# The second piece of a long score row takes the first piece's minimum as its start, and each exponential waits for the reads of its own map

## The reference

```python
def block(args):
    qi, st = args
    sc = jnp.einsum('bhmqd,bhmkd->bhmqk', qi, k).astype(jnp.float32) * scale
    mask = kpos[None, :] <= (st + jnp.arange(Q_BLOCK))[:, None]
    p = jax.nn.softmax(jnp.where(mask, sc, -jnp.inf), axis=-1)
    a = p[:, :, 0] - lam * p[:, :, 1]
    return jnp.einsum('bhqk,bhkd->bhqd', a.astype(v.dtype), v)
```

## Time and profile before

| | us |
|---|---|
| median of the runs | 2307.16 |
| lowest and highest of the 3 | 2304.96, 2308.73 |
| the profiled execution | 2303.62 |
| its span | 2301.7 |
| PE busy in the span | 2207.7 |
| DVE busy | 1846.1 |
| ACT busy | 1121.8 |
| attention, 499 to 845 us of the span | 346.0 |
| PE busy in it | 310.7 |

### The profile page before, as it was taken

How to read it: one execution, slowest core, us unless ns; L and a number is a source line. 1 busy time by engine, 2 the same in 40 slices (tenths; PEclk the granted TensorE clock), 3 DMA queues, 4 the chain that set the end, 5 groups by cost and what they waited for, 6 DMA issues and landing times. The chain is left out here.

```text
span 2301.7 us, 29815 instructions
## 1 busy us (share of the span) xinstructions
PE 2207.7 (96%) x11258; PEld 1853.9 (81%) x11258; DVE 1846.1 (80%) x2593; ACT 1121.8 (49%) x1787; POOL 358.6 (16%) x285
## 2 busy tenths in 40 slices
PE   7999999987999999999999999998999999999998
PEld 4988897866889888878888788887887888878887
DVE  6548796989989886788888998877687777898887
ACT  4532554448888864433334545443343333545452
POOL 0343043833455640000000000000000000000000
PEclk9999999989999999999999999999999999999999
DMA  7441435130000035268888543447234444743434
GB/s 270 160 160 47 147 119 165 37 106 28 15 15 24 10 125 178 88 224 290 280 282 305 184 169 133 173 152 250 101 119 143 154 154 155 255 161 137 169 137 174
DMA packets 185738, 345.10 MB, mean 150 GB/s; under 512 B 11496, under 2 KB 83452, under 8 KB 184572
## 3 DMA queue, kind: packets, MB, share of 16 engines
q1 hardware_dynamic: 185508, 343.16, 43.9%
q10 hardware_dynamic: 88, 0.04, 0.0%
HBM read 236.20 MB, written 106.95 MB: 149 GB/s over the span
## 5 line engine op out<-in xcount | busy, mean ns | idle before, releaser
L2952 PE MATMUL ps<-sb_h_hi 128*128 128x512 f32 x512 | 200.1, 391 | 7.9 <-ACT ps L1710 2.6
L2954 PE MATMUL ps<-sb_h_hi,sb_h_lo 128*128 128x512 f32 x512 | 199.3, 389 | 0.0
L2953 PE MATMUL ps<-sb_h_lo,sb_h_hi 128*128 128x512 f32 x512 | 199.2, 389 | 0.0
L2918 PE MATMUL ps<-sb_h_hi,sb_w_hi 128*128 128x512 f32 x448 | 176.8, 395 | 9.1 <-DVE sb_u_full L2425 9.0
L2601 PE MATMUL ps<-sb_h_hi,sb_w_hi 128*128 128x512 f32 x448 | 177.4, 396 | 0.7 <-DVE sb_w_lo L2235 0.7
L2919 PE MATMUL ps<-sb_h_lo,sb_w_hi 128*128 128x512 f32 x448 | 175.4, 392 | 0.0
L2603 PE MATMUL ps<-sb_h_hi,sb_w_lo 128*128 128x512 f32 x448 | 174.5, 389 | 0.0
L2602 PE MATMUL ps<-sb_h_lo,sb_w_hi 128*128 128x512 f32 x448 | 174.4, 389 | 0.0
L2116 DVE TENSOR_SCALAR_CACHE_REDUCE sb_scores<-ps 128x1024 f32<-128x1024 f32 (+7 forms) x160 | 139.6, 891 | 12.4 <-PE ps L2815 6.9
L2952 PE MATMUL ps<-sb_w_hi 128*128 128x512 f32 x384 | 149.4, 389 | 0.0
L2953 PE MATMUL ps<-sb_w_lo,sb_w_hi 128*128 128x512 f32 x384 | 149.4, 389 | 0.0
(11 more groups left out here) (342 smaller groups left out, 5924.3 us busy)
## 6 DMA issues: line engine op xcount, KB each, us to landing
left_scratch<-sb_u_sum SPq DMA_DIRECT2D x128, 256.0 KB, 5.9
sb_right<-w_gated_scratch SPq DMA_DIRECT2D x16, 2048.0 KB, 8.7
sb_h_lo_full<-left_scratch SPq DMA_DIRECT2D x64, 512.0 KB, 3.8
sb_w_full<-in_w_ff SPq DMA_DIRECT2D x28, 1024.0 KB, 6.3
left_scratch<-sb_u_full SPq DMA_DIRECT2D x96, 256.0 KB, 2.3
sb_w_full<-left_scratch SPq DMA_DIRECT2D x48, 512.0 KB, 3.3
sb_w_raw<-in_w_in SPq DMA_DIRECT2D x16, 1024.0 KB, 6.0
sb_ada<-in_w_ada SPq DMA_DIRECT2D x32, 512.0 KB, 5.3
```

What stands on the lines that cost most here:

```text
L2918: M(psum[:, bank, :], wh[:, k, :], rh[:, k, :], start=fresh and k == 0, stop=False, skip_group_check=True)
L2952: M(dst, hi[:, k, tok], hi[:, 2 + k, :], start=fresh and k == 0, stop=False, skip_group_check=True)
L2953: M(dst, hi[:, k, tok], low[:, 2 + k, :], start=False, stop=False, skip_group_check=True)
L2954: ins = M(dst, low[:, k, tok], hi[:, 2 + k, :], start=False, stop=k == 1, skip_group_check=True)
```

## The change

Three things change.

- In a long unit the read of the second piece passes the first piece's minimum (`part_min[:, s, m, 0:1]`) as the initial value of its own minimum, so that `part_min[:, s, m, 1:2]` is the minimum of the whole row. Since that value is written by an earlier DVE instruction, the read now waits for `sc_read` to have counted it.
- The `TENSOR_REDUCE` into `row_min`, its wait, the tile and the semaphore `max_ready` are gone. `row_shift` takes piece 1 of a long row and piece 0 of a short one.
- Both exponentials of every unit wait for `sc_read`, each for the items of its own map: map 0 for all but the second half of the unit's items, map 1 for all of them.

```diff
         def row_shift(u, m):
 
-            return row_min[:, u % 8, m:m + 1] if u >= FULL else part_min[:, u % 8, m, 0:1]
+            last = int((u // HEADS + 1) * P > WIDE)
+            return part_min[:, u % 8, m, last:last + 1]
+
+        def scores_read(u, m):
+
+            return SC_NO[u + 1] - (0 if m else len(sc_items(u)) // 2)
...
             def exp_of(u, m):
                 n = (u // HEADS + 1) * P
-                if m == 0:
-                    if u < FULL:
-                        act.wait_ge(sc_read, SC_NO[u + 1])
-                    else:
-                        act.wait_ge(max_ready, u - FULL + 1)
+                act.wait_ge(sc_read, scores_read(u, m))
                 A(prob(u, m, 0, n), prob(u, m, 0, n), ACT.Exp, scale=-1.0, bias=row_shift(u, m),
                   accum_out=row_sum(u, m)).then_inc(exp_done, 1)
...
                     else:
+                        begin = None
+                        if c0:
+                            dve.wait_ge(sc_read, r)
+                            begin = part_min[:, s, m, 0:1]
                         dve.wait_ge(sc_mm, r + 1)
-                        V.tensor_scalar(prob(u, m, c0, n), sc_pair(r)[:, 0:n], -SCALE, None, ALU.mult, ALU.min,
+                        V.tensor_scalar(prob(u, m, c0, n), sc_pair(r)[:, 0:n], -SCALE, begin, ALU.mult, ALU.min,
                                         accum_out=part_min[:, s, m, c0 // WIDE:c0 // WIDE + 1]).then_inc(sc_read, 1)
                     r += 1
-                if u >= FULL:
-                    dve.wait_ge(sc_read, SC_NO[u + 1])
-                    V.tensor_reduce(out=row_min[:, s, :], axis=AX.X, op=ALU.min,
-                                    in_=part_min[:, s, :, :]).then_inc(max_ready, 1)
```

More of the change, by code:

```diff
@@ L302, in trunk @@
         part_min = sb("part_min", 207, [P, 8, 2, 2])
-        row_min = sb("row_min", 207.125, [P, 8, 2])
         exp_sum = sb("exp_sum", 207.25, [P, 4, 2, HEADS])
@@ L375, in trunk @@
         split_hi, split_lo = sem("split_hi"), sem("split_lo")
-        sc_mm, sc_read, max_ready, exp_done, a_ready = [sem(n) for n in (
-            "sc_mm", "sc_read", "max_ready", "exp_done", "a_ready")]
+        sc_mm, sc_read, exp_done, a_ready = [sem(n) for n in (
+            "sc_mm", "sc_read", "exp_done", "a_ready")]
         at_mm, at_read, pv_mm, o_read = [sem(n) for n in ("at_mm", "at_read", "pv_mm", "o_read")]
```

## The result

The changed kernel takes 2312.48 us (median of 20 runs, 2306.58 to 2318.28) against 2307.75 us (20 runs, 2300.78 to 2311.39) for the kernel before, run beside it: 4.7 us more. The kernel is slower by more than the 0.2% that can be told. The forecast was 2308.0 us, and its range ended at 2312.

The account below looks back on a forecast made before the run. It took PE or DVE, by stretch, as the limit, with 12.7 us of PE idle in the long units. Terms -1.0 + 0.8 + 0.5 + 1.1 - 0.5 = +0.9 us on 2307.2 gave about 2308.0 us, range 2299 to 2312.

Parts of the forecast that it names:

- the stretches with PE full: Attention at 690 to 737 us and 780 to 822 us: added or saved DVE time meets PE's queue, not its idle time.
- The reduce that goes: End of long units on DVE: 3 reduces at 737 to 780 us on the path, 0.33 us each, 1.0 us gained.
- the bound of 10 us: Upper bound on the removed reduces' gain: 0.33 us of DVE time in each of 32 long units.
- The operand and the wait: Map 0's second piece, 616 to 690 us: operand +0.8, wait +0.5; three units on DVE's path at 737 to 780: +1.1 us.
- The exponentials: Map 0's exponential on ACT starts earlier, may save part of a stall at crowded steps: -0.5 us, bounds 0 and 7.5.
- Rival 1: ACT's lead reaches PE: its turn-read waits except one of 2.0 us go, with one POOL collision; about 2300 us; chance 0.15.
- what can't be summed: `combine`'s small operation takes 1.48 us beside POOL, 0.22 alone; two such shifts allowed, 2.5 us on either side.
- Rival 3: Map 0's second piece, every long unit: start value 0.21 us plus wait 0.12 in the loop; +7, 2314 us; chance 0.13.
- Rival 2: DVE's time is the path and waits are free, outside the stretches with PE full: -3.6, 2303.5 us; chance 0.08.
- The rule against the row: Added waits on DVE: free by the skill's rule, sum 1.2 us lower; 0.12 us each by the trace row, which was used.
- What was to show it: Profile after: no L2121, second pieces 0.06 to 0.07 us longer, ACT's waits under 3 us, long units within 2 us of 206.
- The two signs named as proof of being wrong: 616 to 690 us shrinking by more than 2 us, or second pieces longer by 0.15 us or more.

## Why the prediction was wrong

Two steps failed. The sum charged the start values' operand and wait in too few units, because it took the stretches with PE full as a cover; that is 1.4 us. And it had no term for the granted clock behind PE's waits; that is the larger part of what is left. Of the mechanism, the reduce, the prices and the place in the loop were right. As a difference the forecast was +0.9 us and its range ended at +4.8 over the 2307.16 us of then; the median moved by 4.7 us. So as a difference it is at the range's very end and as a time, 2312.48 us, just above it, where no term of the sum had put it.

**The reduce that goes, -1.0 us.** Right in kind: the loop of the earlier trace rows passes beside it, and the bound of 10 us was far off. Measured -0.5 us in 24 units, and -0.8 us with units 56 and 60 to 62, close to the 1.0 us.

**The operand and the wait, +0.8, +0.5 and +1.1 us.** The prices were right, 0.065 and 0.11 to 0.12 us. So was the place: map 0's second piece is in the loop, map 1's is beside it. The number of units was wrong, and this is the first step that failed. I charged 13 units of 616 to 690 us (they reach n = 1536, not 1408) and 3 later ones, and took the stretches with PE full as a cover. The runs showed 3.0 us in 24 units; with the four others that can be compared (56 and 60 to 62), 3.6 us. That stands against 2.4 us predicted. By stretch, changed kernel against the one with neither: 1.8 us up to 690 us where I had 1.3, 1.0 us in 690 to 737 where I had nothing, 0.5 in 737 to 780 (units 57 and 58 left out) where I had 1.1, and 0.2 in 780 to 822. With the reduces' gain the units give +2.8 us where I had +1.4.

The cover did not exist. A PE busy 46.70 of 47 us looked full, but its score matmul was already waiting for DVE, by so little (0.11 us in this row) that the timeline prints no idle time before it. Kernel before, DVE, then PE, at a unit in that stretch:

```profile
692.29 0.08 DVE L2116 DVE_READ_ACCUMULATOR sb_scores<-ps 128x1 f32 x1
...
693.02 0.16 DVE L2121 TENSOR_REDUCE sb_row_min<-sb_part_min 128x2 f32<-128x4 f32 x1
```

```profile
692.43 0.73 PE L2812 MATMUL ps<-sb_k_stack,sb_q_stack 128*128 128x512 f32 x2
```

The matmul starts 0.14 us after the accumulator read that frees its bank, as it does where PE visibly waits for it: in the earlier trace rows at 626.81, after the read at 626.67. Taken at each of the 31 steps from one long unit to the next, in the kernel before, this distance is 0.13 or 0.14 us in 12 and at most 0.25 in 19. Eight of the 12 show PE waiting, for 0.36 to 0.83 us; four do not, three of them between 686 and 699 us. With slack of 0 to 0.1 us, most of 0.185 us more on DVE goes through. After the change it is 0.15 us or less in 18 steps, and here the wait has become visible (DVE, then PE, of the changed kernel):

```profile
691.40 0.08 DVE L2120 DVE_READ_ACCUMULATOR sb_scores<-ps 128x1 f32 x1
691.51 0.75 DVE L2120 TENSOR_SCALAR_CACHE_REDUCE sb_scores<-ps,sb_part_min 128x512 f32<-128x512 f32 x1
```

```profile
691.53 0.73 PE L2812 MATMUL ps<-sb_k_stack,sb_q_stack 128*128 128x512 f32 x2 [0.26 <-DVE sb_scores L2120]
```

**The exponentials, -0.5 us.** They reach no unit: the long units are the same with and without them (149.51 and 149.54 us), and ACT's waits became waits for PE as foretold. The 0.5 us did not come. Alone, in short units, they even made the kernel slower on both chips (ratios 1.0018 and 1.0014), at a lower mean clock. Rival 1 is out.

**The term that was missing: the clock.** For what can't be summed I had allowed ±2.5 us, for steps of `combine` beside POOL. What came was PE's clock behind PE's waits, which the text did not mention although the 2.5 us stall at unit 57 stood in the profile. Fallen or not, it moves row 14 by 3.2 us, as much as the whole edit in the loop. The units leave 1.9 of the 4.7 us open. The mean clock of the changed kernel is 0.0024 lower than that of the kernel before (0.9857, and 0.9881 in its runs on record), and at 0.7 to 1.4 us per 0.001 that makes 1.7 to 3.4 us, an estimate from the fits above. So the rest goes with the clock. Why the clock is lower stays open; a kernel whose units got shorter (neither start value nor wait) had it as low.

**The rivals.** Rival 3 had the shape of what happened: operand and wait on map 0's second piece in nearly every long unit, the reduce beside the loop. Its price was 0.33 us and I let it decide only from 0.2 us per unit; at 0.185 us, of which 0.13 us on average got through in 28 units, it gives 3.6 us and with the reduces' gain the +2.8. I gave it 0.13. Rival 2 failed on its count: the wait is not free, and the DVE time won was not on the path.

**The rule against the row.** The wait alone cost 1.8 us in 24 units and a gap of 0.11 us at 691.40 to 691.51. The row was right. The Trainium skill, "VectorE: DVE Perf Modes", section "The DRAIN you can't avoid", has a semaphore between chained DVE operations at no extra cost; by that it would have been nothing. The trace disagrees where the second instruction waits for the first one's accumulator. The advice to count operations, which the prediction gives beside it, stands in another section of that page; the count fell by 32 here and the time rose.

**What was to show it.** L2121 is gone; the second pieces are 0.065 us longer and start 0.11 to 0.12 us behind the accumulator read; ACT's waits fell from 28.1 to 1.5 us. All as written. DVE's wait for PE at a unit's end did not grow from 0.54 to 0.8 us: the read that answers to it, at 625.52 us, waits 0.55 us (the record names ACT as its releaser), since map 1's own wait and operand fill the reduce's place. And the long units' stretch was not within 2 us of 206: rows 8 to 13 alone grew by 2.5 us. The two signs named as proof of being wrong (a shorter stretch, second pieces 0.15 us longer) did not come: the forecast failed in a way that they did not cover.

## What to carry to other kernels

Whether a producer is on the path is told by the distance from the instruction that frees a consumer to the consumer's start, unit by unit, and not by the consumer's busy share or its idle column: where the distance is the smallest that occurs, most of what is added went through here, in a stretch that looked full as well. Work that moves from beside a loop into it must be counted in all passes, even when the engine's total falls. And a stall of PE of 2 to 2.7 us in a kernel that is otherwise dense can carry a second price, that of the clock behind it, so two versions are compared by their unit lengths first and by medians of a dozen runs or more, with their mean granted clock, second. A small effect that profiles seem to show is sorted by chip as well as by kernel.

## What the runs showed of the hardware

- The granted clock may or may not fall behind the same wait of PE: 2.50 us, ending between 769 and 774 us, with the clock staying at 1.00 in one profile of the kernel before and at 0.50 from 770 to 776 us in another. Behind a 2.1 us wait that ended at 839 us it stood at or near 0.50 for over 10 us in one profile (0.64, 0.50, 0.50 in 838 to 853 us), and at 1.00 behind the same wait, 1.95 us and ending at 832 us, in another of the same kernel.
- A [P, 1] start value adds 65 ns to a reduction with accumulator, at 128 columns (285 to 351 ns) as at 1024 (1219 to 1284).
- A DVE instruction that waits for the accumulator of the one before it starts 0.11 to 0.12 us after the start of the accumulator read (691.40 to 691.51 us); without the wait the two start together (690.77 us). The matmul of PE that such a read releases starts 0.13 to 0.14 us after it at the least (692.29 to 692.43 us).
- A one-column memset of 0.06 us, ready beside a long read, costs DVE no time (24 units within 0.02 us); eight such memsets that wait for one another take 0.94 us, 0.12 us each.
